# A gate expansion of rank 16: one float32r pass over stacked high and low parts in place of a float32 product

## What is computed

```python
proj = h @ w_in[l]
(g_q, g_k, g_v, g_r, g_og, m_cq, m_ckv, m_kr, gate_a, gate_b) = jnp.split(proj, offsets, axis=-1)
gate_logit = (g_r @ gla_w_gate_up[l] + gla_b_gate[l]).astype(jnp.float32)   # g_r: (1, 1024, 16), weight: (16, 512)
log_a = jax.nn.log_sigmoid(gate_logit) / GLA_TAU
o = _gla_chunked(g_q, g_k, g_v, log_a)     # chunks of 64 tokens, 4 heads of 128 keys and 256 values
```

## Time and profile before

| | us |
|---|---|
| runs | 1780.34, 1781.61, 1781.75 |
| median of the runs | 1781.61 |
| span of the profiled execution | 1780.1 |
| PE busy in it | 1750.3 |
| DVE busy | 1017.8 |
| POOL busy | 813.4 |
| ACT busy | 751.9 |

### The profile page before, as it was taken

One profiled execution on the slowest core, in us unless ns is written; L12 is line 12 of the kernel. 1 busy time (PEld: TensorE's weight loads), 2 busy tenths in 40 slices (PEclk: granted clock), 3 DMA queues, 4 the chain that ended last, 5 costly groups with the idle time before them and its releaser, 6 DMA issues.

```text
span 1780.1 us, 23407 instructions
## 1 busy us (share of the span) xinstructions
PE 1750.3 (98%) x8464; PEld 1457.9 (82%) x8464; DVE 1017.8 (57%) x1749; ACT 751.9 (42%) x1398; POOL 813.4 (46%) x668
## 2 busy tenths in 40 slices
PE   8999999999999999999999999999999999999998
PEld 6788887888988877788888888878888888888886
DVE  6313411634445269455464634587777775798798
ACT  6534433344343313545453102664444444444442
POOL 6888754321122254233342356697777677500000
PEclk9999999999999999999999999999999999999999
DMA  5433425214122087722342552434334443495333
GB/s 167 138 107 113 124 77 175 60 48 84 60 71 96 29 272 247 211 85 81 101 148 96 171 201 71 166 107 154 113 113 147 148 146 110 165 342 186 100 95 118
DMA packets 217135, 233.29 MB, mean 131 GB/s; under 512 B 24317, under 2 KB 147373, under 8 KB 217021
## 3 DMA queue, kind: packets, MB, share of 16 engines
q1 hardware_dynamic: 181406, 167.57, 30.5%
q10 hardware_dynamic: 35616, 64.24, 10.3%
HBM read 160.19 MB, written 71.58 MB: 130 GB/s over the span
## 4 chain that ended last, share of the span: by engine, by line
PE 82%; DVE 7%; DMA 4%; ACT 2%; issue 2%; POOL 1%; SPq 1%; ACTq 0%; DVEq 0%; POOLq 0%
PE psum_all L1190 23%; PE psum_all L1192 23%; PE psum_all L1191 23%; PE psum_all L1518 2%; DMA ga_st<-d_sga 1%; PE psum_all L1534 1%; PE psum_all L1535 1%; PE psum_all L1536 1%; PE psum_all L1254 1%; PE psum_all L1258 1%; PE psum_all L1506 1%; PE psum_all L1504 1%; PE psum_all L1507 1%; PE psum_all L1505 1%; PE psum_all L1503 1%
## 5 line engine op out<-in xcount | busy, mean ns | idle before, releaser
L1068 POOL CAST w_hi<-w_raw 128x512 fp32r<-128x512 f32 (+3 forms) x82 | 66.9, 816 | 336.2 <-PE psum_all L1192 330.9
L1190 PE MATMUL psum_all<-xT_hi,w_hi 128*128 128x512 f32 (+1 forms) x456 | 182.8, 401 | 5.1 <-POOL w_lo L1004 3.3
L1192 PE MATMUL psum_all<-xT_hi,w_lo 128*128 128x512 f32 (+1 forms) x456 | 180.0, 395 | 0.0
L1191 PE MATMUL psum_all<-xT_lo,w_hi 128*128 128x512 f32 (+1 forms) x456 | 179.6, 394 | 0.0
L1070 POOL TENSOR_TENSOR w_lo<-w_raw,w_hi 128x512 fp32r<-128x512 f32 (+3 forms) x82 | 144.3, 1759 | 6.7
L1190 PE MATMUL psum_all<-t_hi,w_hi 128*128 128x512 f32 x352 | 137.4, 390 | 1.3 <-DVE r L2255 0.4
L1192 PE MATMUL psum_all<-t_hi,w_lo 128*128 128x512 f32 x352 | 137.0, 389 | 0.0
L1191 PE MATMUL psum_all<-t_lo,w_hi 128*128 128x512 f32 x352 | 137.0, 389 | 0.0
L1130 POOL TENSOR_TENSOR w_lo<-w_raw,w_hi 128x512 fp32r<-128x512 f32 x88 | 115.3, 1318 | 41.0 <-ACT w_hi L3038 40.9
L1084 POOL TENSOR_SCALAR p_sb<-p_sb,small 128x128 f32<-128x128 f32 (+3 forms) x64 | 48.1, 751 | 162.6 <-DVE small L2110 162.5
L1130 POOL TENSOR_TENSOR w_lo<-s_sb,w_hi 128x512 fp32r<-128x512 f32 x66 | 88.1, 1339 | 47.7 <-ACT w_hi L3038 47.7
(11 more groups left out here) (553 smaller groups left out, 5015.2 us busy)
## 6 DMA issues: line engine op xcount, KB each, us to landing
w_raw<-in_w_up_dram SPq DMA_DIRECT2D x44, 512.0 KB, 5.0
fa_raw<-d_f SPq DMA_DIRECT2D x76, 256.0 KB, 2.7
w_raw<-in_w_in_dram SPq DMA_DIRECT2D x36, 512.0 KB, 4.7
d_f<-up_g SPq DMA_DIRECT2D x44, 256.0 KB, 3.2
d_f<-f_sum SPq DMA_DIRECT2D x33, 256.0 KB, 2.6
wd<-in_w_down_dram SPq DMA_DIRECT2D x33, 256.0 KB, 4.7
w_raw<-in_w_out_dram SPq DMA_DIRECT2D x8, 1024.0 KB, 5.0
x_tok<-in_x_dram SPq DMA_DIRECT2D x8, 512.0 KB, 6.7
```

The lines of the kernel that those rows point to most:

```text
L1068: wc.done(nc.gpsimd.tensor_copy(w_hi[b][:, w], src[:, w]))
L1190: pe.matmul(out_ap, ah, bh, start=start and i == 0, stop=False, skip_group_check=more)
L1191: pe.matmul(out_ap, ah, bl, start=False, stop=False, skip_group_check=more)
L1192: last = pe.matmul(out_ap, al, bh, start=False, stop=stop and i == len(terms) - 1, skip_group_check=more)
```

## The change

The 16 rows of `g_r` are produced four times, on partitions 0 to 16, 16 to 32, 96 to 112 and 112 to 128 (`RANKS`), and the weight of the expansion gets 128 rows. Rows 0 to 96 of `rk_fm` hold the high part of the products' output, rows 96 to 128 the low part. `w_gate` holds the weight's high part on rows 0 and 96 and on, its low part on rows 16 and 112 and on, and zeros on the rotary key's rows. One float32r product over all 128 rows then sums high x high, high x low, low x high and low x low.

```diff
-        w_gate = put("w_gate", (RANK, GH * DK), 88)
+        w_gate = put("w_gate", (P, GH * DK), 88, F32R)
+        wg_raw = put("wg_raw", (P, GH * DK), 88)
+        wg_hi, wg_lo = put("wg_hi", (P, GH * DK), 56, F32R), put("wg_lo", (P, GH * DK), 58)
-        rk_fm = put("rk_fm", (P, S), 40)
+        rk_fm = put("rk_fm", (P, S), 40, F32R)
+        rk_kr = put("rk_kr", (96, S), 60)
...
-        slot(("rk", 0), KT, 224, (0, 32, win[:, :, C_R:C_R + 32]), (32, ROPE, win[:, :, C_KR:C_KR + ROPE]),
-             (96, P, win[:, :, C_CQ + 512:C_CQ + 640]))
+        slot(("rk", 0), KT, 256, (0, 32, win[:, :, C_R:C_R + 32]), (32, ROPE, win[:, :, C_KR:C_KR + ROPE]),
+             (P, P, win[:, :, C_CQ + 512:C_CQ + 640]))
...
-        PARAMS = 12
+        PARAMS = 15
+        RANKS = (0, RANK, 96, 96 + RANK)
...
-                    sp.dma_start(w_gate[:, :], gla_w_gate_up[0]).then_inc(par_landed, 16)
+                    sp.wait_ge(consts, 15)
+                    for row in RANKS:
+                        sp.dma_start(wg_raw[row:row + RANK, :], gla_w_gate_up[0]).then_inc(par_landed, 16)
...
+            ms.done(nc.gpsimd.memset(wg_raw[:, :], 0.0))
+            ms.done(nc.gpsimd.memset(is_hi, 0.0))
+            ms.done(nc.gpsimd.memset(is_lo, 1.0))
+            ms.wait()
+            for row in RANKS[0::2]:
+                ms.done(nc.gpsimd.memset(small[row:row + RANK, 56:57], 1.0))
+                ms.done(nc.gpsimd.memset(small[row:row + RANK, 57:58], 0.0))
+            ms.wait()
...
+                    if n == 0:
+                        rank = raw(0, KT, 256)
+                        for row in RANKS[1:]:
+                            wc.done(nc.gpsimd.tensor_copy(rank[:, :, row:row + RANK], rank[:, :, 0:RANK]))
+                        wc.wait()
...
-                    pe.matmul(bank(kind), w_gate[:, h * DK:(h + 1) * DK], rk_fm[0:RANK, half * HALF:(half + 1) * HALF],
+                    pe.matmul(bank(kind), w_gate[:, h * DK:(h + 1) * DK], rk_fm[:, half * HALF:(half + 1) * HALF],
                               start=True, stop=True).then_inc(mm, 1)
...
             pe.wait_ge(*ev_at[gid[("rk", 0, 1)]])
+            pe.wait_ge(sm["gate_in"], 3)
             gates(0)
...
-                    last = pe.transpose(bank(kind)[:, i * 96:(i + 1) * 96], rk_fm[0:96, t * P:(t + 1) * P], ident[0:96, 0:96])
+                    last = pe.transpose(bank(kind)[:, i * 96:(i + 1) * 96], rk_kr[:, t * P:(t + 1) * P], ident[0:96, 0:96])
...
+            def rank_low(half):
+                hs = slice(half * HALF, (half + 1) * HALF)
+                ve.wait_ge(sm["rk_hi"], half + 1)
+                split_lo(rk_fm[96:P, hs], bank(("rk", 0, half))[96:P, :], rk_fm[96:P, hs]).then_inc(sm["gate_in"], 1)
+
+            ve.wait_ge(sm["up_mm"], XPRODUCTS)
+            ve.wait_ge(par_landed, 16 * PARAMS)
+            op(V.tensor_copy(wg_hi[:, :], wg_raw[:, :]))
+            op(split_lo(wg_lo[:, :], wg_raw[:, :], wg_hi[:, :]))
+            op(V.tensor_scalar(wg_hi[:, :], wg_hi[:, :].bitcast(F32), is_hi, None, ALU.mult))
+            V.scalar_tensor_tensor(w_gate[:, :], wg_lo[:, :], is_lo, wg_hi[:, :].bitcast(F32), ALU.mult, ALU.add).then_inc(sm["gate_in"], 1)
+            rank_low(0)
+            rank_low(1)
             ve.wait_ge(sm["par_mm"], 1)
...
-            A.copy(rk_fm[0:96, 0:HALF], got(("rk", 0, 0))[0:96, :]).then_inc(ev_a, 1)
+            def rank_out(half):
+                src, hs = got(("rk", 0, half)), slice(half * HALF, (half + 1) * HALF)
+                A.copy(rk_fm[:, hs], src).then_inc(sm["rk_hi"], 1)
+                A.copy(rk_kr[0:96, hs], src[0:96, :]).then_inc(ev_a, 1)
```

More of the change, by code:

```diff
@@ L169, in block_kernel @@
         ms_tok = small[:, 40:40 + 2 * TT]
+        is_hi, is_lo = small[:, 56:57], small[:, 57:58]
         rs_b = [put("rs_bq", (P, S), 68), put("rs_bk", (P, S), 28)]
@@ L520, in block_kernel @@
                  "rot_ok kst3_ok sins angs s_mm nb_ok p_exp p_norm t_mm pt_hi pt_lo pv_mm om_ev pj_mm pj_hi pj_lo "
-                 "mo_mm mo_ev mix_ok ln_n ln_r ln2_n ln2_r ln2_g ln2_end mix_hi mix_lo wo_mm wo_ev ln_v ln_s "
+                 "mo_mm mo_ev mix_ok ln_n ln_r rk_hi gate_in ln2_g ln2_end mix_hi mix_lo wo_mm wo_ev ln_v ln_s "
                  "hT_mm up_mm fs_hi fs_lo dn_mm dn_ev ln2_v ln2_s ln2_ok ad2 vd2 "
@@ L1336, in _ @@
             pe.wait_ge(*x_out(last_m, "C11", 0))
-            feature_group(("rk", 0, 0), ("rk", 0), 0, 96, 0)
+            feature_group(("rk", 0, 0), ("rk", 0), 0, P, 0)
             pe.wait_ge(*xp("b12_lo", QK - 1))
             pe.wait_ge(*x_out(last_m, "C12", 0))
-            feature_group(("rk", 0, 1), ("rk", 0), 0, 96, 1)
+            feature_group(("rk", 0, 1), ("rk", 0), 0, P, 1)
             pe.wait_ge(*x_out(last_m, "C21", 0))
-            feature_group(("rk", 1, 0), ("rk", 0), 96, P, 0)
+            feature_group(("rk", 1, 0), ("rk", 0), P, P, 0)
             pe.wait_ge(par_landed, 16 * PARAMS)
@@ L1353, in _ @@
                     t = 4 * half + i
-                    last = pe.transpose(bank(kind)[:, i * 96:(i + 1) * 96], rk_fm[0:96, t * P:(t + 1) * P], ident[0:96, 0:96])
+                    last = pe.transpose(bank(kind)[:, i * 96:(i + 1) * 96], rk_kr[:, t * P:(t + 1) * P], ident[0:96, 0:96])
                 last.then_inc(mm, 1)
-            feature_group(("rk", 1, 1), ("rk", 0), 96, P, 1)
+            feature_group(("rk", 1, 1), ("rk", 0), P, P, 1)
             for j in range(4):
@@ L2742, in square @@
                 A.activation(dst[:, :], lat_fm[c][:, :], ACT.Square).then_inc(sm["lat_sq"], 1)
[L2744 removed]
+            def rank_out(half):
+                src, hs = got(("rk", 0, half)), slice(half * HALF, (half + 1) * HALF)
+                A.copy(rk_fm[:, hs], src).then_inc(sm["rk_hi"], 1)
+                A.copy(rk_kr[0:96, hs], src[0:96, :]).then_inc(ev_a, 1)
+            rank_out(0)
             for i in range(2):
@@ L2748, in _ @@
                 ac.dma_start(lat_fm[c][:, :], d_lat[c * P:(c + 1) * P, :]).then_inc(lat_in, 16)
-            A.copy(rk_fm[0:96, HALF:S], got(("rk", 0, 1))[0:96, :]).then_inc(ev_a, 1)
+            rank_out(1)
             A.copy(lat_fm[4][:, 0:HALF], got(("rk", 1, 0))).then_inc(ev_a, 1)
```

## The result

| | before | after |
|---|---|---|
| runs (us) | 1780.34 to 1781.75 (4) | 1770.98, 1771.5, 1772.0, 1773.52 |
| median | 1781.15 | 1771.75 |
| span of the profiled execution | 1780.1 | 1771.8 |

The changed kernel takes 0.9949 of the time before, 95% interval 0.9937 to 0.9961: 6.9 to 11.2 us less. 1773.6 was predicted, with 1771.0 to 1777.8 as the range.

What follows compares the result with a forecast made beforehand. TensorE's own time was taken as the bound. Savings of 5.05 us at the expansions plus 3.1 for the clock, less 0.15, gave 8.0 us off the median of 1781.61: 1773.6 us, range 1771.0 to 1777.8.

Steps and rivals of the forecast that it cites:

- Uses 2 to 4: Second to fourth gate expansion with the first weight product behind: 2.24 us becomes 0.79, saving 1.45 each, 4.35 in all.
- The first use: First gate expansion: saves 0.7 us of 1.3, as TensorE then waits for ScalarE's second read of the PSUM bank.
- The clock: Behind two of the four expansions the half-clock falls were taken as gone: 1.55 us each, 3.1 for both.
- rival B: Both clock falls behind the expansions stay, since TensorE shows no idle gap ahead; gain 4.9, time 1776.7, chance 0.2.
- Added work at 0: Added GpSimd copies and split, VectorE operations, ScalarE copies and SP DMAs were all said to stay hidden: 0 us.
- rival D: Slower: GpSimd's strided copies decide when slot 0 is ready; whole gain used up at 3.3 us each; chance 0.03.
- Groups of 128 rows at 0: TensorE's ("rk", 0, half) groups produce 128 rows instead of 96, at 0.23 us per product either way: 0 us.
- What is late next: Transposes of o_tok behind the third and fourth use wait for VectorE's scaling: 0.15 us taken off for both.

Runs made afterwards that it cites:

- f32_rows96: Kernel before, with the float32 expansion over 96 rows instead of 16, zeros in the added weight rows; 1777.34 us, ratio 0.9986.
- The two pairs: Expansion products repeated: float32 twice over 16 rows (1792.94 us) against 96 (1783.41); float32r eight times over 16 (1793.98) against 128, the changed kernel's (1786.13).
- f32_rows16_twice: Kernel before, with each float32 product of the expansion over 16 rows issued twice in a row; 1792.94 us, ratio 1.0078.
- after_swap: Changed kernel with the eight rotary key transposes ahead of the first expansion, ScalarE's order to match; 1770.19 us, ratio to the kernel before 0.9948.
- pad_only: Kernel before, with slot 0 padded from 224 to 256 columns and two GpSimd copies, float32 expansion kept; 1779.53 us, ratio 0.9998.
- after_again: The changed kernel unaltered, run again beside the kernel before; 1770.86 us, ratio to the kernel before 0.9956.
- x8 kernels: One-pass float32r expansion, each product issued eight times: over 16 rows without low parts, 1793.98 us; over 128 rows in the changed kernel, 1786.13 us.

## Why the prediction was right, by its own steps

**Uses 2 to 4** were sized exactly from the expansion on, 0.79 us and 1.45 saved each; the neighbour's rows were the right ones to take. The 2.24 of the float32 stretch hold a part that the prediction did not name, the late load behind 16 rows (f32_rows96: 1.96). The same thing ahead of the use it left out of the sum: the step into it went from 0.26 to 0.08 us, 0.5 for the three.

**The first use** gave 0.63 where 0.7 was said, with a wait of 0.55 for ScalarE where 0.6 was said (305.9 to 306.5). The chain of two reads of one bank was the right thing to look at: by TensorE's own time alone 1.3 would have been promised.

**The clock.** Both falls went, at 1.61 and 1.65 us where 1.55 was said, so the forecast held against rival B. By the idle gaps that the Trainium skill names (TensorE: Matmul & The Clock Gate, Why this matters for your kernels) they should have stayed. The two pairs decide it: with TensorE busy throughout, repeated products over 16 rows bring half clock at three and four of four uses, over 96 and 128 rows at none. Another fall of this kernel has idle time ahead of it, as the Trainium skill (same page and section) has it: behind the wait for `c_lo` the clock is 0.51 from 677.30 to 680.70 in the trace of before (9 products in 3.4 us), with TensorE idle for 2.56 us ahead of it. That the idle time is its cause was not tested, and its length does not decide alone: at the same place there is no fall behind 2.22 us in f32_rows16_twice, and one behind 1.83 in after_swap.
What the prediction had wrong is that it took the two falls of one trace as a property of the kernel. Their number differs between executions, from none (pad_only) to two. The part of the stage's gain that does not hang on them is 8.87 - 1.61 - 1.65 = 5.6 us. The medians were 9.4 apart on the first chip and 7.6 on that of after_again, which leaves 3.8 and 2.0. That would be 2.3 and 1.2 falls at 1.65, an inference from medians and not a count: in the profiled executions the part behind the stage alone varies from 1108.2 to 1113.3 us. That the two falls of one trace come near what the clock gave on the first chip is luck in part.

**Added work at 0.** GpSimd, VectorE, ScalarE and SP were hidden, as said. The three copies took 0.76 us together, where the row of 128 x 160 gave 1.0 (rival D needed 3.3 each). The split of slot 0 ended at 287.66, not at 286.3, because in this execution all of it stood 1.5 later; TensorE came at 288.99, 1.3 behind it. VectorE was slow beside GpSimd's slot 1, as foreseen: a subtraction of 128 x 512 with two operands took 2.26 us, and the next operation 4.71, to 296.65, when GpSimd's low part (291.45 + 4.93) had just ended; the one behind it took 0.75. Two of the four were thus dearer than the 1 us allowed to each; they still ended at 297.4, within the 298.4 that was said, and 4.4 us of margin were left at the sixth.

**Groups of 128 rows at 0.** Here the step was off: "0.23 at both widths" hid 0.232 against 0.227, and the row length of the slot was not looked at. Over 72 products and the group behind them this is 0.5 us in favour of the change.

**What is late next.** The place was right and the size too small: TensorE waits for VectorE's scaling of `o_tok` behind the third and the fourth use, 0.23 and 0.22 us, and loses 0.5 in all where 0.15 was taken off. To count the third use alone was right: from slot 0 on, the scaling came 4.3 us earlier than before, as much as TensorE had gained up to that use. But the use gave 3.3 us and not 3.0 (the step into it and the dearer fall), and the weight load that waits stands 0.11 ahead of the transpose (439.14 against 439.25 in the trace of before).
The terms left out (0.5 and 0.5) and the one too small (0.35) partly cancel: the stage gave 8.9 against the 8.0 of the sum, and the span 8.3. The predicted 1773.6 lies 1.85 above the median measured, about the size of one fall.

## What to carry to other kernels

A product that uses few rows of the array costs more than its own columns: where TensorE is the bound, look at the granted clock behind each such stretch and at the start of the next weight load, before asking what the product itself takes. Filling the rows with something useful (low parts here) or even with zeros in the weight removed both costs here. One profiled execution that has such a fall shows what it is worth, but not how many an average execution has, and one without a fall proves little; an experiment that makes the suspected stretch longer shows more than either.
When a stretch of TensorE shrinks, follow the PSUM bank's next user back through its readers: 0.55 us of the gain stayed there, and taking that wait out only moved it to VectorE's next deadline. Look at waits of the weight loads too: the two of 0.2 us for `o_tok` stand in the lines of PEld and not in those of PE.

## What the hardware showed that was not expected

- Half clock comes with stretches of few-row products though TensorE is not idle ahead of it: 3.6 us or more of products over 16 rows brought it at 7 of 8 uses in two profiled executions (at 5 of the 7 it began while they still ran), 1.9 us of them at 2 of 4 in one and 0 of 4 in another, and as long a stretch over 96 or 128 rows at 0 of 8.
- The longer few-row stretches brought longer half-clock stretches: 3.4 us each with 1.9 us of them, 6.8 at 5 of the 7 with 3.6.
- The Trainium skill (TensorE: Matmul & The Clock Gate, Why this matters for your kernels) says that a single product over 32 rows takes the same time as one over 128. For the product itself the traces agree at 16 rows: in the x8 kernels the products follow each other every 0.227 us over 16 rows as over 128. The switches are what costs: 0.20 us more back to 128 rows in float32r (0.99 against 0.79), and 0.17 more into the 16 (0.26 against 0.08).
- Weight products of 96 columns went at 0.232 us out of rows of 224 and at 0.230 out of rows of 256, those of 128 columns out of rows of 256 at 0.227.
